# The even mixer's output projection as sixteen tiles in a ring of four banks, with its conformer half beside the scan output's turn, skip, gate and norm

## The reference

```python
def ssd_readout(y, xs, z, d_skip, norm_g):
    b, n = y.shape[0], y.shape[1]
    y = y + d_skip.astype(jnp.float32)[:, None] * xs.astype(jnp.float32)
    y = y.reshape(b, n, SSD_INNER) * jax.nn.silu(z.astype(jnp.float32))
    return rmsnorm(y, norm_g)

# in even_mixer
o_ssd = ssd_readout(ys_l[0] + ys_l[1], xs_l, pl[..., :SSD_INNER], d_skip, ssd_g)
o_cf = conformer_conv(pl[..., cf0:cf0 + CF_CH], pl[..., cf0 + CF_CH:], cf_w, cf_b, cf_lng, cf_lnb, rows)
y_lat = (jnp.concatenate([o_ssd, o_cf.astype(o_ssd.dtype)], axis=-1) @ w_out).astype(hl.dtype)
# in second_block
xl = xl + m_l[:, 2] * y_l
```

## Time and profile before

| | |
|---|---|
| median of three runs | 2803.73 us (2803.44 to 2804.33) |
| the profiled execution | 2807.14 us, its span 2804.9 us |
| PE busy | 2425.3 us (86%), mean granted clock 0.920 of full |
| DVE busy | 1121.1 us (40%) |
| ACT busy | 531.7 us (19%) |
| DMA | 487.21 MB, mean 174 GB/s |
| scan's last DVE instruction to the projection's first matmul | 1479.39 to 1514.91 us |
| the projection's matmuls | 1514.91 to 1627.15 us |

### The profile page before, as it was taken

One profiled execution on the slowest core, in us unless ns is written; L12 is line 12 of the kernel. 1 busy time (PEld: TensorE's weight loads), 2 busy tenths in 40 slices (PEclk: granted clock), 3 DMA queues, 4 the chain that ended last, 5 costly groups with the idle time before them and its releaser, 6 DMA issues. The chain is left out here.

```text
span 2804.9 us, 35626 instructions
## 1 busy us (share of the span) xinstructions
PE 2425.3 (86%) x14207; PEld 1646.6 (59%) x14207; DVE 1121.1 (40%) x2402; ACT 531.7 (19%) x1033; POOL 48.8 (2%) x45
## 2 busy tenths in 40 slices
PE   7999857797997689998865969999969989869996
PEld 6878757786886534455853444444427556745543
DVE  1464124312001269983763034545440445223322
ACT  0123311101000110023300021111121655121111
POOL 0000012100000000000000000000000000000000
PEclk9999879998999799998877979999979999879998
DMA  7442563142441412553002239997942121369995
GB/s 239 144 135 91 199 230 121 41 140 90 150 158 56 150 60 85 201 180 136 1 0 105 75 118 384 383 391 276 389 185 90 62 74 62 135 257 380 387 380 207
DMA packets 304156, 487.21 MB, mean 174 GB/s; under 512 B 12882, under 2 KB 183940, under 8 KB 303876
## 3 DMA queue, kind: packets, MB, share of 16 engines
q1 hardware_dynamic: 290672, 467.12, 46.7%
q10 hardware_dynamic: 11604, 11.68, 1.5%
q0 software_dynamic: 1728, 6.29, 0.6%
HBM read 468.80 MB, written 16.25 MB: 173 GB/s over the span
## 5 line engine op out<-in xcount | busy, mean ns | idle before, releaser
L1788 PE MATMUL bank<-hn,weights 128*128 128x512 f32 x640 | 279.3, 596 | 8.3 <-PEq L164 8.3
L1788 PEld LDWEIGHTS bank<-hn,weights 128*128 128x128 f32 x640 | 121.5, 191 | 159.0 <-issue 158.9
L2914 PE MATMUL bank<-hn,weights 128*128 128x512 f32 (+1 forms) x512 | 175.4, 501 | 20.8 <-ACT forget L2825 18.0
L1861 DVE SCALAR_TENSOR_TENSOR conv_sum<-mixer_then_weights_ahead,vec,conv_sum 128x572 f32<-128x572 f32 x240 | 174.8, 810 | 0.0
L482 PE MATMUL bank<-u,weights 128*128 128x256 f32 x768 | 171.0, 379 | 1.4 <-PEq L164 1.4
L2497 PE MATMUL bank<-hn,expert_out 64*128 64x512 f32 (+1 forms) x656 | 157.9, 559 | 14.5 <-DVE x_both L3035 8.2
L2486 PE MATMUL bank<-weights,gathered 128*64 128x256 f32 x1344 | 161.4, 384 | 6.3 <-DMA weights<-in_moe_w_up 3.4
L3034 DVE SCALAR_TENSOR_TENSOR x_both<-bank,mod,x_both 128x256 f32<-128x256 f32 x184 | 88.2, 479 | 191.9 <-PE bank L2497 191.8
L482 PEld LDWEIGHTS bank<-u,weights 128*128 128x128 f32 x768 | 145.1, 190 | 25.2 <-issue 6.5
L1433 PE MATMUL bank<-u,weights 128*128 128x256 f32 x704 | 154.7, 383 | 4.9 <-PEq L164 4.9
L2914 PEld LDWEIGHTS bank<-hn,weights 128*128 128x128 f32 x512 | 98.3, 195 | 90.5 <-issue 62.1
(11 more groups left out here) (502 smaller groups left out, 3398.2 us busy)
## 6 DMA issues: line engine op xcount, KB each, us to landing
weights<-in_mod_w SPq DMA_DIRECT2D x48, 1024.0 KB, 7.3
weights<-in_moe_w_gate SPq DMA_DIRECT2D x42, 1024.0 KB, 9.6
weights<-in_moe_w_up SPq DMA_DIRECT2D x42, 1024.0 KB, 10.7
weights<-in_moe_w_down SPq DMA_DIRECT2D x42, 1024.0 KB, 10.5
weights<-in_w_in SPq DMA_DIRECT2D x36, 1024.0 KB, 5.0
weights<-in_ab_w_in SPq DMA_DIRECT2D x20, 1024.0 KB, 5.1
mixer_then_weights_ahead<-in_moe_w_gate SPq DMA_DIRECT2D x20, 1024.0 KB, 9.7
mixer_then_weights_ahead<-in_moe_w_up SPq DMA_DIRECT2D x20, 1024.0 KB, 10.7
```

The source lines that it names most:

```text
L1788: last = pe.matmul(tile_bank(n)[:, :], unit[:, k, lane * P:(lane + 1) * P], hn[:, k, :], start=k == 0, stop=k == DC - 1)
L1861: ins = dve.scalar_tensor_tensor(s, x, w, s, ALU.mult, ALU.add)
L2914: last = pe.matmul(bank, units[key][:, k, lane * P:(lane + 1) * P], hn[:, k, cols], start=k == 0, stop=k == DC - 1)
```

## The change

The four stages become one, `even_output`. The weights `ab_w_out_2` are planned as 8 units of 8 row tiles by 256 columns in place of 2 row tiles by 1024 columns: first the four of the conformer half, then the four of the scan half, again 1 MB each but in rows of 1 KB where they had 4 KB. The projection becomes sixteen tiles of 8 matmuls each (one unit feeds two tiles) in the ring of banks 0 to 3: tiles 0 to 7 are the conformer half of the 8 output tiles, tiles 8 to 15 the scan half. Each tile is added to `x_both` when it is ready, so the residual runs twice for every output tile. Banks 4 to 7 serve the turn, the sums and the spread roots. The skip reads the turned scan output straight from the bank, so the turn's copies are gone, and all 8 squares are on ACT.

```diff
-    feed.plan(1, 8, lambda i, j: out[:, 2 * j:2 * j + 2, :])
+    feed.plan(1, 8, lambda i, j: out[:, (DC, 0)[j // 4]:(DC, 0)[j // 4] + DC, WIDE * (j % 4):WIDE * (j % 4) + WIDE])
...
-        turn(kit, [([y[:, t, c * P:(c + 1) * P] for t in range(NT)], out[:, c, :]) for c in range(DC)])
...
-        vector_only(kit, skip_and_gate)
-    rmsnorm(kit, out, [(slice(0, T2), lambda c: out[:, c, :], lambda c: kit.col("ssd_norm_g_2", c), None, None)])
+def even_output(kit, y, xbc, z, so, cf, residual, loads):
...
+            @block.sync
+            def _(sp):
+                sp.wait_ge(gated, DC)
+                loads(sp)
+                feed.run(sp, ready, [2 * j + 2 for j in range(tiles // 2)])
...
+                def turns(first):
+                    for c in range(first, first + HALF):
+                        if c >= HALF:
+                            pe.wait_ge(skipped, c - HALF + 1)
+                        for t in range(T2 // P):
+                            last = pe.transpose(turn_bank(c)[:, t * P:(t + 1) * P], y[:, t, c * P:(c + 1) * P], kit.c("ident"))
+                        last.then_inc(turned, 1)
+
+                def project_tile(n, unit, x, after_scaling=False):
+                    if n >= 4:
+                        pe.wait_ge(evacuated, n - 3)
+                    for k in range(DC):
+                        if after_scaling:
+                            pe.wait_ge(scaled, k + 1)
+                        last = pe.matmul(kit.bank[n % 4][:, 0:T2], unit[:, k, (n % 2) * P:(n % 2 + 1) * P], x(k), start=k == 0, stop=k == DC - 1)
+                    last.then_inc(ready, 1)
...
+                beside = {0: lambda: turns(HALF), 1: sums, 2: spread_roots}
+                turns(0)
+                for n in range(tiles):
+                    if n % 2 == 0:
+                        unit = feed.arrive(pe, (DC, WIDE))
+                    if n < DC:
+                        project_tile(n, unit, lambda k: cf[:, k, :])
+                    else:
+                        project_tile(n, unit, lambda k: so[:, k, :], n == DC)
+                    if n in beside:
+                        beside[n]()
...
+                skip_and_gate(0)
+                add(0)
+                skip_and_gate(HALF)
+                add(1)
+                dve.wait_ge(summed, 1)
+                dve.tensor_scalar(rstd[:, :], total, 1.0 / D, EPS, ALU.mult, ALU.add).then_inc(mean_ready, 1)
+                dve.wait_ge(root_ready, 1)
+                dve.reciprocal(rstd[:, :], rstd[:, :]).then_inc(inverted, 1)
+                add(2)
+                dve.wait_ge(spread, 1)
...
+                for c in range(DC):
+                    dve.scalar_tensor_tensor(so[:, c, :], so[:, c, :], kit.col("ssd_norm_g_2", c), root, ALU.mult, ALU.mult).then_inc(scaled, 1)
+                for n in range(3, tiles):
+                    add(n)
```

More of the change, by code:

```diff
@@ L2206, in ssd, with _, sums, spread_roots @@
-        vector_only(kit, skip_and_gate)
-    rmsnorm(kit, out, [(slice(0, T2), lambda c: out[:, c, :], lambda c: kit.col("ssd_norm_g_2", c), None, None)])
+def even_output(kit, y, xbc, z, so, cf, residual, loads):
+    nc = kit.nc
+    feed = kit.feed
+    FOURTH = T2 // 4
+    tiles, HALF = 2 * DC, DC // 2
+    with ExitStack() as mem:
+        sq = mem.enter_context(kit.sb("squares", [P, DC, T2]))
+        rstd = mem.enter_context(kit.sb("rstd", [P, FOURTH]))
+        with stage(nc, "turned", "skipped", "gated", "squared", "summed", "mean_ready", "root_ready", "inverted", "spread", "scaled", "ready", "evacuated", "v") as (
+                block, turned, skipped, gated, squared, summed, mean_ready, root_ready, inverted, spread, scaled, ready, evacuated, vsem):
+            turn_bank = lambda c: kit.bank[4 + c % 4]
+            total, root = kit.bank[4][:, 0:FOURTH], kit.bank[5][:, 0:T2]
+            @block.sync
[3 more added lines that the diff above has]
+                feed.run(sp, ready, [2 * j + 2 for j in range(tiles // 2)])
+            @block.tensor
+            def _(pe):
+                def turns(first):
[13 more added lines that the diff above has]
+                    last.then_inc(ready, 1)
+                def sums():
+                    pe.wait_ge(skipped, DC)
+                    for c in range(DC):
+                        pe.wait_ge(squared, c + 1)
+                        for g in range(4):
+                            last = pe.matmul(total[32 * g:32 * g + 32, :], kit.c("ones")[:, 0:32], sq[:, c, g * FOURTH:(g + 1) * FOURTH],
+                                             start=c == 0, stop=c == DC - 1)
+                    last.then_inc(summed, 1)
+                def spread_roots():
+                    pe.wait_ge(inverted, 1)
+                    for g in range(4):
+                        last = pe.matmul(root[:, g * FOURTH:(g + 1) * FOURTH], kit.c("ident")[:, 32 * g:32 * g + 1].broadcast_to([P, P]),
+                                         rstd[:, :], start=True, stop=True)
+                    last.then_inc(spread, 1)
+                beside = {0: lambda: turns(HALF), 1: sums, 2: spread_roots}
[9 more added lines that the diff above has]
+                        beside[n]()
+            @block.scalar
+            def _(act):
+                act.activation(rstd[:, 0:1], kit.c("ones")[:, 0:1], ACT.Sqrt)
+                for c in range(DC):
+                    act.wait_ge(gated, c + 1)
+                    act.activation(sq[:, c, :], so[:, c, :], ACT.Square).then_inc(squared, 1)
+                act.wait_ge(mean_ready, 1)
+                act.activation(rstd[:, :], rstd[:, :], ACT.Sqrt).then_inc(root_ready, 1)
+            @block.vector
+            def _(dve):
+                v = Signal(vsem)
+                def skip_and_gate(first):
+                    for c in range(first, first + HALF):
+                        dve.wait_ge(turned, c + 1)
+                        dve.scalar_tensor_tensor(so[:, c, :], xbc[:, c, :], kit.col("ssd_d_2", c), turn_bank(c)[:, :], ALU.mult, ALU.add).then_inc(skipped, 1)
+                    for c in range(first, first + HALF):
+                        dve.wait_ge(skipped, c + 1)
+                        dve.tensor_tensor(so[:, c, :], so[:, c, :], z[:, c, :], ALU.mult).then_inc(gated, 1)
+                def add(n):
+                    dve.wait_ge(ready, n + 1)
+                    if n >= DC:
+                        dve.wait_ge(evacuated, n - DC + 1)
+                    residual(dve, v, n % DC, kit.bank[n % 4][:, 0:T2]).then_inc(evacuated, 1)
+                skip_and_gate(0)
[8 more added lines that the diff above has]
+                dve.wait_ge(spread, 1)
+                dve.wait_ge(gated, DC)
+                dve.wait_ge(squared, DC)
+                for c in range(DC):
+                    dve.scalar_tensor_tensor(so[:, c, :], so[:, c, :], kit.col("ssd_norm_g_2", c), root, ALU.mult, ALU.mult).then_inc(scaled, 1)
+                for n in range(3, tiles):
+                    add(n)
@@ L3023, in residual @@
                 return e.scalar_tensor_tensor(x2[:, c, LAT], ps[:, LAT], m(2, c, 1), x2[:, c, LAT], ALU.mult, ALU.add)
-            project_down(kit, lambda k: so[:, k, :] if k < DC else cf[:, k - DC, :], T2, [2] * 8, residual,
-                         before=load_first_ahead(kit, inp, 0, ahead, range(free_early)))
+            y = hn[:, :, :].rearrange("p c t -> p (c t)").rearrange("p (t d) -> p t d", t=T2 // P)
+            even_output(kit, y, xbc, z, so, cf, residual, load_first_ahead(kit, inp, 0, ahead, range(free_early)))
         shifts(kit, mod, 4, "norm_ffn_g_2", 0, gain)
```

## The result

The changed kernel takes 2780.38 us (median of 4 runs, 2773.97 to 2783.62), the one before 2804.03 us beside it: a ratio of 0.991 with the interval [0.9891, 0.993], 23.7 us less. Run twice more on other occasions it took 2780.65 and 2781.20 us, against 2808.28 and 2806.95 us for the kernel before, ratios of 0.9904 [0.9878, 0.993] and 0.9907 [0.9891, 0.9924]. The forecast was 2777.2 us with the range 2773 to 2785.

The account below looks back on a forecast made before the run. A 34.3 us DVE/ACT/PE chain with barriers, then a PE-bound projection of 112.3 us. Merged: 118.9 + 0.5 + 0.9 + 1.45 = 121.75 against 148.25 us, so 2803.73 - 26.5 = 2777.2 us, range 2773 to 2785.

Parts of the forecast that it names:

- The sum on PE: PE's work from first transpose to last matmul of the merged stage: 118.9 us, ending near 1599.5.
- The 0.5 us for the switches: Five switches between kinds of matmul on PE, where the array may run empty, at 0.1 us each.
- The 0.3 us put in for the last sum's way: Landing time of the last sum pass, added to 1.7 us for 64 passes, making 2.0 us.
- the wait of tile 8: Tile 8 needs the eight scalings: done by 1516, asked for 38 us later near 1545.
- The tail: After the last matmul: residual 0.88 us, then a barrier clearing 13 semaphores at about 0.07 each, 1.45 us.
- The one called tightest: PE's sums wait for the eighth square: ready at 1498.2, asked for at 1500.2, slack 2 us.
- The gain: First transpose to next stage's first DVE instruction: 148.25 us before, 121.75 after, 26.5 us gained.
- 3 us on each side: Range allowance for TensorE's clock rising and falling elsewhere in the short stages behind the stretch; nothing put in the sum.
- Rival 1: Mixed beginning: clock falls or waits on PE give back up to 7.4 us, 2784.6 us; 12%.
- Rival 2: Tiles 4 to 15: bank waits keep TensorE at half clock, up to 2859 us; 3%.
- Rival 3: Experts' stage: weight loads slip into it at 2.7 us each; three give 2785 us; 3%.
- Rival 4: Merged stage: an overlooked wait prevents the overlap, 2803 us or somewhat less; 2%.

Follow-up runs that it names:

- the padding test: Changed kernel with three or nine extra DVE multiplications between tile 0's residual and the second four skips: stretch 121.11 us with three, 124.24 us with nine.
- ring_alone: Kernel before with only the projection made sixteen tiles in a four-bank ring, conformer half first, 1 KB weight rows: ratio 0.9997, stretch 148.24 us.
- a further fusion: Changed kernel with the next norm moved into the same stage: 2778.76 us with sums between tiles, 2775.96 us with all sums behind the last tile.

## Why the prediction was right

- *The sum on PE.* Forecast 118.9 us plus 0.5 for switches, 1599.5 as the end; measured from 1479.02 to 1597.74, where PE's last record ends, 118.7. By pieces: turn 3.65 and tile 0 7.4 (3.7 and 7.3), second turn and tile 1 8.62 (8.61), sums and tile 2 8.95 (8.86), spread and tile 3 7.76 (8.06), then twelve tiles in 82.40, 6.87 each (6.86). TensorE's clock rose at about 1483.5, 4.5 us after the start, as forecast (0.74 stands in the window from 1483 to 1484). The 0.5 us for the switches is the term that was too large: the first four tiles with the pieces ahead of them take 36.4 us, and the forecast has 36.5 for them without any switch, the spread 0.3 under its price and the sums 0.1 over theirs. The 0.3 us put in for the last sum's way, which no row had shown, comes out: 64 passes at 0.027 are 1.7 us, and the block adds 2.09 to a tile. In the wait of tile 8 the 38 us was a slip: from 1516 to 1545 there are 29 us, and the wait was as harmless as that says.
- *The tail.* Residual 0.88 and barrier 1.49 (1.45); the price a clear, 0.07 by two rows, is 0.071 by the test.
- *The waits.* Every slack held. The one called tightest was 1.9 us wide (2), but "were it 2 us later PE would stand" was too strict: by the padding test 3.4 us are covered, because seven eighths of the sums can be done before the last square is there.
- *The gain.* 27.1 us in the stretch, 26.5 forecast. The median moved by 23.7, 27.6 and 25.7 us on the three occasions; the forecast's 2777.2 lies 3.2 to 4.0 us below the medians. That difference is not in the stretch. It is where I put 3 us on each side, in the part ahead of it and behind it, whose length differs from execution to execution. The median of 2780.38 lies just above the 2774 to 2780 that got 80%. That it came so near is in part luck: the median of the kernel before alone was between 2804.03 and 2808.68 us on the four occasions, and with 2808.28 as its base the same sum would have said 2781.8. What the traces bear out is the gain in the stretch.
- *Rival 1* (clock or waits in the mixed beginning) did not happen: PEclk is 1.00 from 1490 to 1597.7, with PE busy 107.70 of the 107.70 us, and PE's rows have no brackets. *Rival 2* (the ring keeps the clock down) did not happen: clock 1.00 and 40.00 of 40 us in the ring's window, and ring_alone costs nothing. The swing between the two clock levels that the Trainium skill tells of a bf16 kernel cycling through PSUM banks at 512 columns ("TensorE: Matmul & The Clock Gate", section "A second HAM failure mode: psum-queue depth-cycling"), no run here shows; the matmuls here are float32. DVE is idle 5.99 of each 6.86 us, so a bank is free long before PE comes to it. *Rival 3*: the experts' first matmul comes 46.93 us after the stretch, 47.25 before, and the loads are there. *Rival 4* (no overlap) did not happen either: tiles 0 to 2 run between the pieces, at 1482.46, 1491.60 and 1500.45.
- *What the text told too simply.* It spoke as if the gain were the conformer half's work laid over an idle chain. The experiments split the 27.1 us otherwise: 15.9 come with the merged stage even if the scan's half goes first (no barriers, no copies, gates and squares beside each other, tiles beginning at the first scaling, of which only the last was told apart), 2.45 from having tiles that need no scaling at all, 8.8 from the three tiles between the pieces. The sum was right because it counted PE's work, whatever the reason that it became continuous. It also counted that work at full clock almost throughout, and the 5.1 us by which PE's records take less time come with that; the text gave this part of the gain no name.

## What to carry to other kernels

When stages alternate between an engine that waits and an engine that works, walk along the engine that will bound the merged stage, add up only its own passes, and check for each of its waits how early it is over; the others' work need not be summed. Where that engine's small pieces can stand in one block, measure that against spreading them: six groups of eight small sums between large matmuls had a price of their own, which ate 3.1 of the 4.0 us that a further fusion could bring. It is no general price of a switch: the second turn, sixteen transposes between two tiles, cost 1.76 us, where four groups at 0.435 are 1.74. And before crediting the reordering, try the merged stage without it: here more than half of the gain needed no reordering.

## What was new about the hardware

- Eight passes of 128 columns with 32-column weights cost PE 0.56 us between two tiles of 512-column matmuls, six times alike, but 64 of them in one block 2.1 us, 0.27 for eight. The extra 0.3 us a group is not explained by these runs; sixteen transposes between two tiles show no such extra (1.76 us against 1.74).
- Closing a stage of this program costs 0.071 us for every semaphore it clears, measured by thirteen that nothing used (0.78 us at DVE with three, 1.49 with thirteen, 2.41 with twenty-six).
- The part of the program behind the stretch, with the same instructions in the same order, took from 1172.3 to 1182.5 us, several times the 2.1 us by which the first pair of profiles differ there. By whole runs the theories above could not have been told apart where they differ by less than that; the stretch between two fixed instructions repeats within 0.02 us.
